# Two attentions in which the scalar engine takes the next tile's exponential before it rounds turned blocks

## The reference, cut to what matters

```python
def attend(qb):
    s = jnp.einsum('bqhgd,bkhd->bhgqk', qb, k, preferred_element_type=jnp.float32) * scale
    p = jax.nn.softmax(s, axis=-1).astype(v.dtype)
    return jnp.einsum('bhgqk,bkhd->bqhgd', p, v)
```

## Time and profile before

| what | value |
|---|---|
| median of 3 runs | 2350.7 us (2349.38 to 2351.59) |
| the profiled execution | 2355.96 us |
| its span | 2354.1 us |
| TensorE busy | 2294.0 us (97%) |
| vector, scalar, GpSimd busy | 1244.9, 899.2, 1254.3 us |
| attention of layer 0, first to last exponential | about 304 to 430 us |
| attention of layer 1, the same | about 1386 to 1560 us |

### The profile page before, as it was taken

The page is one execution under the profiler, slowest core; times in us unless marked ns, Lnnn a source line. Parts: engine busy times, 40 slices in busy tenths (PEclk is TensorE's granted clock), DMA queues, the critical chain, the costliest instruction groups (busy, mean ns, idle before and its releaser), DMA issues.

```text
span 2354.1 us, 37608 instructions
## 1 busy us (share of the span) xinstructions
PE 2294.0 (97%) x14575; PEld 2091.3 (89%) x14575; DVE 1244.9 (53%) x2000; ACT 899.2 (38%) x1893; POOL 1254.3 (53%) x1066
## 2 busy tenths in 40 slices
PE   8999989999999999999999998999999999999998
PEld 8999878999999999999998778888878888888887
DVE  5221567459444444444449558865954444444444
ACT  5125656445322222222225456754532222222222
POOL 1344388545455555555533338864555555555561
PEclk9999989999999999999999999999999999999999
DMA  5131001422111111111112000023211111111112
GB/s 207 46 125 46 23 19 64 143 86 68 50 55 46 50 55 55 50 55 46 46 55 62 28 6 2 2 81 92 74 54 50 54 54 50 50 51 53 54 54 76
DMA packets 187937, 137.46 MB, mean 58 GB/s; under 512 B 7409, under 2 KB 176642, under 8 KB 187762
## 3 DMA queue, kind: packets, MB, share of 16 engines
q1 hardware_dynamic: 187632, 134.97, 18.6%
q10 hardware_dynamic: 130, 0.09, 0.0%
HBM read 121.89 MB, written 12.85 MB: 57 GB/s over the span
## 4 chain that ended last, share of the span: by engine, by line
PE 81%; DVE 8%; POOL 4%; issue 3%; ACT 2%; DMA 0%; SPq 0%; DVEq 0%; ACTq 0%; POOLq 0%
PE PS L164 26%; PE PS L166 26%; PE PS L165 26%; PE PS L2077 1%; DVE b_lo L2781 1%; PE PS L2045 1%; POOL tmp L1904 1%; POOL rope L1904 1%; DVE x_raw L2777 1%; DVE stat L2160 0%; DVE w_lo L2137 0%; DVE x_hi L2808 0%; DVE x_lo L216 0%; DVE t L2801 0%; POOL w_lo L470 0%
## 5 line engine op out<-in xcount | busy, mean ns | idle before, releaser
L2475 POOL TENSOR_TENSOR w_lo<-stage,w_hi 128x512 fp32r<-128x512 f32 x374 | 506.6, 1358 | 613.6 <-ACT w_hi L2471 611.3
L2471 ACT ACTIVATE w_hi<-stage 128x512 fp32r<-128x512 f32 x374 | 233.1, 628 | 558.5 <-PE PS L166 558.5
L2874 DVE TENSOR_TENSOR hT<-hT,PS 128x528 f32<-128x528 f32 (+1 forms) x384 | 267.0, 696 | 309.0 <-PE PS L166 308.3
L164 PE MATMUL PS<-s_hi,w_lo 128*128 128x264 f32 (+1 forms) x1104 | 354.5, 321 | 4.1 <-DVE s_lo L2820 3.1
L164 PE MATMUL PS<-x_hi,w_lo 128*128 128x264 f32 (+2 forms) x1092 | 352.6, 323 | 5.6 <-POOL w_lo L470 2.2
L166 PE MATMUL PS<-s_hi,w_hi 128*128 128x264 f32 (+1 forms) x1104 | 354.0, 321 | 0.0
L165 PE MATMUL PS<-s_lo,w_hi 128*128 128x264 f32 (+1 forms) x1104 | 352.8, 320 | 0.0
L166 PE MATMUL PS<-x_hi,w_hi 128*128 128x264 f32 (+2 forms) x1092 | 351.7, 322 | 0.0
L165 PE MATMUL PS<-x_lo,w_hi 128*128 128x264 f32 (+2 forms) x1092 | 351.2, 322 | 0.0
L164 PE MATMUL PS<-b_hi,w_lo 128*128 128x264 f32 (+1 forms) x864 | 278.5, 322 | 1.4 <-DVE a L2884 1.4
L165 PE MATMUL PS<-b_lo,w_hi 128*128 128x264 f32 (+1 forms) x864 | 277.7, 321 | 0.0
(11 more groups left out here) (376 smaller groups left out, 4937.7 us busy)
## 6 DMA issues: line engine op xcount, KB each, us to landing
stage<-in_ffn_w SPq DMA_DIRECT2D x280, 256.0 KB, 2.8
stage<-in_even_w_out SPq DMA_DIRECT2D x32, 256.0 KB, 2.7
stage<-in_odd_w_out SPq DMA_DIRECT2D x32, 256.0 KB, 2.7
stage<-in_mla_w_in SPq DMA_DIRECT2D x12, 512.0 KB, 7.0
stage<-in_gqa_w_qkv SPq DMA_DIRECT2D x12, 512.0 KB, 3.6
h_spill<-hT SPq DMA_DIRECT2D x8, 528.0 KB, 5.1
hT<-h_spill SPq DMA_DIRECT2D x8, 528.0 KB, 7.4
conv_hi<-s_hi SPq DMA_DIRECT2D x4, 528.0 KB, 2.7
```

Of the source, the lines that this page charges most:

```text
L164: T.matmul(out, a_lo, b_hi, start=first, stop=False)
L2471: A.activation(ring(w_hi, n), source(n), ACT.Copy).then_inc(rounded, 1)
L2475: G.tensor_tensor(ring(w_lo, n), source(n), ring(w_hi, n).bitcast(F32), ALU.subtract).then_inc(split, 1)
L2874: V.tensor_tensor(o, o, sums(st.slot), ALU.add).then_inc(drained, 1)
```

## The change

Only scalar's loop over the steps changes. Before, a step rounded its items, then the block of tile n-2, and then took the exponential of tile n; only step 2 of layer 1 had the exponential first. After, each step has the exponential first, in both layers. The call that goes with it, `wait_exponentials`, moves along: in layer 0 it waits in step 1 for rotated keys, in layer 1 in step 2 for rotated queries. `finish` stays ahead of both, and the tail's rounding and the rounding of values stay behind.

```diff
                     if n >= lag + 3 and closes_output(n - lag - 3):
                         finish(n - lag - 3)
-                    eager = not L0 and n == 2
-                    if eager:
+                    if n < len(tiles):
                         first_steps.wait_exponentials(act, n)
                         exponentials(n)
                     for what in items_at.get(n - 1, []):
                         round_item(what)
-                    if eager:
+                    if not L0 and n == 2:
                         first_steps.scalar_at(act, n)
                     if lag <= n < len(tiles) + lag:
                         round_bank(("p", n - lag, 0))
                     if n < len(tiles):
-                        if not eager:
-                            first_steps.wait_exponentials(act, n)
-                            exponentials(n)
                         if n == (1 if L0 else 2):
```

## The result

The changed kernel takes 2438.1 us (median of 4 runs, 2434.0 to 2440.2), 1.0368 times the kernel before (95% interval 1.0355 to 1.0381). The profiled execution took 2437.1 us with a span of 2435.3, 81.2 more than the span before. The forecast was 2433. By the medians the change costs 87.4 us; the two profiled executions lie closer together because that of the kernel before took 5.3 us more than its median, while that of the changed kernel took 1.0 less than its own.

What follows compares the result with a forecast made beforehand. TensorE was taken as the bound, 97% busy, with vector close behind. Layer 1 +49, layer 0 +25 and the clock +8 summed to +82, so 2350.7 + 82 = 2433 us; 8-in-10 range 2398 to 2470.

Steps and rivals of the forecast that it cites:

- The relay: Both attentions: maximum, exponential, rounding, split, reciprocal, next maximum form a closed loop once per tile; as summed, chance 0.67.
- Layer 1: Layer 1's attention: a unit's steps add to 12.8 us against 9.15, 15.1 with new keys; +49 in all.
- Layer 0 at full clock: Layer 0's attention: five steps per unit, 3.2, 3.85, 3.9, 4.9 and 4.1, sum 20.0 us; +25 in all.
- The first tiles: Layer 0's first tiles, partly waiting for GpSimd and late norms: 0.5 a step over seven steps, 3.5 us.
- TensorE's busy share: Sign in the changed profile: TensorE's busy share in both attentions near 70%, its time waiting for vector's splits.
- The clock: Both attentions: five more spells of lower TensorE clock at 1.6 us each, +8; bounds 0 and 38.
- rival A: Both attentions: the clock falls once or more in each unit, 38 instead of 8, 2463 us; chance 0.14.
- the sentence that differences carry over: Profiled execution was 5.3 us over the median; differences were carried to the median: 2350.7 + 82 = 2433.
- B: Relay partly covered: turns after query blocks and output copies not late, some 16 us less, no clock term, 2409; chance 0.10.
- C: Layer 1, faster: exponential fills scalar's waits for turns, tails split 0.37 us earlier, 18 us, 2333; chance 0.06.
- D: No difference, 2351 us: scalar's order is hidden under GpSimd or TensorE; chance 0.03.
- The rival of late splits in the banks: Late splits of turned banks hold TensorE wherever the maximum stands: changed kernel 2430 or more, kernel before 5 to 30 slower.

Runs made afterwards that it cites:

- the filled run: Changed kernel, with TensorE making extra score products, overwritten afterwards, in the long wait of layer 0's step 3 (five tiles): 2430.3 us, ratio 1.0331.
- the version built on it: Kernel before, with the repeated tail rounded right behind its block and ahead of the exponential: 2346.2 us, ratio 0.9982.
- the early maximum: Vector takes the maximum of tile n+1 ahead of its splits of step n: changed kernel 2427.8 us, kernel before 2429.7 us.

## Why the prediction was right

**The relay** was the right mechanism. Two pairs show it: with the link from maximum to exponential cut, the order costs 4 us instead of 87; and 0.09 us put on the loop 104 times costs 8.7 us in the changed kernel and 0.6 in the one before.

**Layer 1.** Forecast 2.8, 3.3, 3.4, 3.3 for the steps, measured 2.73, 3.40, 3.33, 3.40; forecast 3.9 and 5.1 ahead of new keys, measured 4.00 and 4.97. From tile 16 to tile 60: 145.4 forecast, 146.0 measured. The tail's split doesn't start one pitch, 0.60, behind the block's, but 0.72 (1569.09 to 1569.81), so tail steps were forecast 0.1 too short. From the last split to the next maximum there are 0.68 and not 0.75 (1566.37 to 1567.05), since the reciprocal no longer waits for an exponential; so the other two were forecast 0.07 too long. These nearly cancel. The other tiles gave 9.0 where I had 10.5. In all +48.1 against +49. With the spell of 6.8 us out of the side before, it would be about +50: the run with the change in layer 0 alone had 171.64 us in this layer, without a fall.

**Layer 0 at full clock.** 3.2, 3.85, 3.9, 4.9 and 4.1 were forecast, sum 20.0; with the wait filled they measure 3.24, 3.84, 3.92, 4.77 and 4.26, sum 20.04. The first tiles cost 3.3 (3.5 forecast), the last four steps 2.4 (2.5 forecast). TensorE's busy share is the one sign that was off: 77% in both attentions, where I wrote near 70%. I had divided the 8.9 us of before by the longer unit, but the same work reads 9.73.

**The clock** is the term that was mis-sized, by 2 us. I took five more spells in both layers at 1.6 us each, +8. In layer 0's attention there were seven, after three before, nearly one in each unit, and at least one per unit was what rival A said. The units of tiles 10 to 34 took 110.4 us where the relay alone makes 100.2, so the spells cost 10.2 there, of which the filled run gave 7.8 back. A spell of 3.4 us costs a unit 1.6, as forecast (21.6 against 20.0 us), but two of the five lasted 6.8 us and cost 2.7 each (22.8). In layer 1, where rival A said the same, there were two, against one before, and here they cost nothing: a unit with new keys takes 15.1 us with or without one. So A held in one layer and not in the other. Between the two profiled executions the parts are 24.4 for the relay in layer 0 (25 forecast), 10.2 for the clock (8), 48.1 for layer 1 (49) and -1.5 for the rest (0): 81.2 against 82.

**The 5 us that are missing** against the median are not in the sum but in the sentence that differences carry over. The profiled execution of the kernel before lay 5.3 us over its median, and I carried its times over as if the changed kernel's would lie as high. They didn't, as said with the result. So the closeness of 81.2 to 82 is partly luck: against other executions of the same code in these layers the change costs about 36 and 50 us, not 34.6 and 48.1.

The page's sentence about back-to-back batches (Trainium skill, Perfetto Trace Analysis, Matmul Optimizations) agrees with layer 0's trace, where TensorE worked 0.69 of 3.0 us and the next 3.5 us ran at 0.53 on average, and not with layer 1's steady units, where it worked 9.73 of 12.9 us at 1.00. Layer 1's two falls stand in units with new keys, behind stretches with less work:

```profile
1471.90:1475.30 3.40, 1.48 (x12) 1.30 (x12) 2.06 (x5) 2.03 (x5) 2.63 (x4) 1.00 0.00 0
1475.30:1478.70 3.40, 3.40 (x15) 3.00 (x16) 1.96 (x5) 1.35 (x4) 2.23 (x5) 0.50 0.00 0
```

**The other rivals.** B is refuted by the steps: the turn behind a query block stayed late (4.97 in layer 1, 4.77 in layer 0, where B had 3.6 and 3.7), and so did the output's copy (3.92, where B had 3.2). C would have needed the maximum before the turn; its own term, the tail's rounding close behind its block, is real, and the version built on it gained 0.2% in the order of before. D is refuted by the time. The rival of late splits in the banks, which I wrote down with the runs, is what the early maximum ran into: it is a second loop beside the first, and it becomes the bound when the first is opened in the wrong place.

**What stays open.** What a spell costs was measured only for units of layer 0, by adding work, and when the clock falls and when it doesn't is not settled: the third unit with new keys ran at full clock. And why the changed order with the cut still costs 4 us, all of it in layer 0.

## What to carry to other kernels

Where two in-order engines hand work back and forth, write down for each step who waits for whom in both queues, and look for a circle. A reorder adds no work and can still close one; its length is the sum of the starts-to-starts along it, and these can be read from the trace of the kernel before. Here the instruction that waits for the other engine's newest result belonged behind those that wait for older ones, and the orders that took the exponential or the maximum earliest were the slow ones.

## What the runs showed of the hardware

- A one-column scalar instruction has a row of 0.19 us but takes up 0.09 of the engine: the steps grew by 0.09. The Trainium skill (Perfetto Trace Analysis, Optimizing Scalar/DVE Operations) says of an instruction's fixed data-access overhead that its profiled latency is about twice the busy time, since the half that acknowledges the write overlaps the next instruction; the trace agrees for this instruction, which is hardly more than that overhead, 0.19 against 0.09.
- A wait of 2.3 us (0.69 us of work in 3.0) was followed by 3.4 us at the lower clock. Layer 1's 224 us, 77% busy and with waits for splits of 1.7 us at most, kept the higher one but for two spells of 3.4 us. The first of these two stands behind waits of 1.56 and 1.15 us (1.48 us of work in 3.4), so one long wait isn't needed for a fall. Adding 1.9 us of useless products in each of five waits of layer 0 made the kernel 7.8 us faster.
